# Experts take 96 rows as three 32-column strips of plain float32 weights on TensorE's four column tiles, with no split of expert slabs and a 14-slab ring

## The reference, cut to what matters

```
logits = (h @ w_router) + b_router
top_v, top_i = lax.top_k(logits, 2)
gates = softmax(top_v)
for e in range(8):
    y = (silu(h @ w1[e]) * (h @ w3[e])) @ w2[e]     # w1, w3: 1024 x 3584, w2: 3584 x 1024
    out = out + dense_gate[..., e:e+1] * y
```

## Time and profile before

| | us |
|---|---|
| median of three runs | 1696.49 |
| profiled execution, first to last instruction (span) | 1693.5 |
| time of that execution, as far as it is known: median less span | 3.0 around the span |
| ahead of the experts | 713.1 |
| eight experts | 713.1 to 1672.0 |
| behind the experts | 21.5 |

### The profile page before, as it was taken

How to read it: one execution, slowest core, us unless ns; L and a number is a source line. 1 busy time by engine, 2 the same in 40 slices (tenths; PEclk the granted TensorE clock), 3 DMA queues, 4 the chain that set the end, 5 groups by cost and what they waited for, 6 DMA issues and landing times.

```text
span 1693.5 us, 22933 instructions
## 1 busy us (share of the span) xinstructions
PE 1587.1 (94%) x8697; PEld 1295.9 (77%) x8697; DVE 1255.3 (74%) x1097; ACT 982.6 (58%) x885; POOL 153.9 (9%) x135
## 2 busy tenths in 40 slices
PE   6889999799899887899999999999999999999996
PEld 3579999498785574488888888888888888888874
DVE  4355543578782834488898888988888888889996
ACT  2244432433322633277777877877877877777774
POOL 0000000025541511200000000000000000000210
PEclk9789999899999988599999999999999999999998
DMA  9895555855458428689999999999999999999991
GB/s 345 295 346 177 180 160 183 299 174 194 155 212 305 141 75 333 214 320 382 359 389 384 355 395 364 380 387 379 370 391 367 378 386 364 382 386 363 394 386 49
DMA packets 248254, 512.28 MB, mean 302 GB/s; under 512 B 9046, under 2 KB 68614, under 8 KB 248176
## 3 DMA queue, kind: packets, MB, share of 16 engines
q1 hardware_dynamic: 241015, 490.27, 80.6%
q0 software_dynamic: 4768, 16.89, 2.5%
q10 hardware_dynamic: 2400, 4.17, 0.7%
HBM read 498.19 MB, written 13.82 MB: 302 GB/s over the span
## 4 chain that ended last, share of the span: by engine, by line
PE 76%; DVE 9%; DMA 5%; POOL 3%; ACT 3%; issue 3%; SPq 1%; DVEq 0%; ACTq 0%; POOLq 0%
PE wide L474 22%; PE wide L475 22%; PE wide L476 22%; DVE w_lo L1729 2%; POOL phase L1907 2%; DMA ring<-in_ada_mix_w 2%; DVE phase L1570 2%; DMA ring<-in_ada_ffn_w 1%; PE wide L930 1%; POOL phase L1913 1%; ACT w_hi L1262 1%; PE wide L525 1%; PE wide L536 1%; SPq L437 1%; DMA ring<-in_cache_v 1%
## 5 line engine op out<-in xcount | busy, mean ns | idle before, releaser
L1729 DVE TENSOR_TENSOR w_lo<-ring,w_hi 128x2048 fp32r<-128x2048 f32 x336 | 767.6, 2290 | 114.0 <-ACT w_hi L1262 112.5
L1262 ACT ACTIVATE w_hi<-ring 128x2048 fp32r<-128x2048 f32 x336 | 643.6, 1919 | 216.5 <-PE wide L476 214.3
L474 PE MATMUL wide<-w_hi,xe_hi 128*128 128x512 f32 x896 | 355.7, 397 | 5.6 <-DVE w_lo L1729 2.9
L475 PE MATMUL wide<-w_lo,xe_hi 128*128 128x512 f32 x896 | 350.2, 391 | 0.0
L476 PE MATMUL wide<-w_hi,xe_lo 128*128 128x512 f32 x896 | 350.2, 391 | 0.0
L474 PE MATMUL wide<-tHi,w_hi 128*128 128x264 f32 x672 | 198.3, 295 | 20.4 <-DVE mLo L1488 20.4
L404 DVE TENSOR_TENSOR w_lo<-ring,w_hi 128x2048 fp32r<-128x2048 f32 (+1 forms) x58 | 139.0, 2399 | 101.2 <-ACT w_hi L1002 100.9
L475 PE MATMUL wide<-mLo,w_hi 128*128 128x264 f32 x736 | 212.3, 288 | 0.0
L474 PEld LDWEIGHTS wide<-w_hi,xe_hi 128*128 128x128 f32 x896 | 169.0, 189 | 45.1 <-DVE w_lo L1729 8.6
L476 PEld LDWEIGHTS wide<-w_hi,xe_lo 128*128 128x128 f32 x896 | 168.8, 188 | 35.8
L475 PEld LDWEIGHTS wide<-w_lo,xe_hi 128*128 128x128 f32 x896 | 169.0, 189 | 33.4
(11 more groups left out here) (313 smaller groups left out, 1709.8 us busy)
## 6 DMA issues: line engine op xcount, KB each, us to landing
ring<-in_moe_w SPq DMA_DIRECT2D x336, 1024.0 KB, 7.4
ring<-in_ffn_w SPq DMA_DIRECT2D x30, 1024.0 KB, 5.4
ring<-in_ada_mix_w SPq DMA_DIRECT2D x24, 1024.0 KB, 8.8
ring<-in_ada_ffn_w SPq DMA_DIRECT2D x24, 1024.0 KB, 12.0
ring<-in_w_q SPq DMA_DIRECT2D x12, 1024.0 KB, 9.1
ring<-in_cache_k SPq DMA_DIRECT2D x24, 512.0 KB, 4.9
ring<-in_cache_v SPq DMA_DIRECT2D x24, 512.0 KB, 6.3
ring<-in_w_kv SPq DMA_DIRECT2D x8, 1024.0 KB, 6.5
```

Source lines behind the costliest of these rows:

```text
L474: pe.matmul(out, a[0], b[0], start=start, stop=False, skip_group_check=True)
L475: pe.matmul(out, a[0], b[1], start=False, stop=False, skip_group_check=True)
L1262: act.activation(w_hi[:, (NSPLIT + k) % PAIRS, :], ring[:, slot, :], ACT.Copy).then_inc(hi_done, 1)
L1729: dve.tensor_tensor(w_lo[:, i, :], ring[:, slot, :], w_hi[:, i, :].bitcast(F32), ALU.subtract).then_inc(lo_done, 1)
```

## The change

SLOTS goes from 128 to 96, and the 96 rows of an expert are three strips of 32. PASSES stays 3, as 264/96 rounds up to 3, and the flag's bound becomes 96.5. Experts' weights are no longer split: TensorE reads the plain float32 slabs. A group is four matmuls with the same 128x32 stationary strip; each takes a quarter of the slab's columns and writes one of four 32-partition tiles of a bank.

w1 and w3 are taken in two parts, columns 0-2047 (four times 512) and 2048-3583 (four times 384); w2 in slabs of 256 rows by 1024 columns (four times 256). An expert has 38 slabs: 16 of 1 MB, 8 of 1.5 MB, 14 of 1 MB; a row of a slab is 8, 6 or 4 KB long in DRAM, where it was 2 KB (w1, w3) or 4 KB (w2). The ring for them is 14 MB: the room of w_hi, w_lo, the old ring and xT, in one piece.

```
-SLOTS = 128
+SLOTS = 96
+STRIPS = SLOTS // 32
+PARTS = ((0, 512), (2048, 384))
+UNITS = 56
...
+    eslabs = [(m, 0, k) for m in (1, 3) for k in range(KC)] + [(m, 1, k) for m in (1, 3) for k in range(KC // 2)]
+    eslabs += [(2, 0, k) for k in range(FE // (2 * P))]
...
+                def product(m, part):
+                    first, n = 0 if m == 1 else STRIPS, PARTS[part][1]
+                    for k in range(KC):
+                        i, kk = eslabs.index((m, part, k // (part + 1))), k % (part + 1)
+                        if kk == 0:
+                            landed(i)
+                        for s in range(STRIPS):
+                            for j in range(4):
+                                mm = pe.matmul(bank[first + s][32 * j:32 * (j + 1), 0:n], xe[:, k, 32 * s:32 * (s + 1)], expert_slab(i)[:, kk, n * j:n * (j + 1)],
+                                               start=(k == 0), stop=(k == KC - 1))
+                        if kk == part:
+                            mm.then_inc(expert_used, 1)
+                        if (m, part, k) == (1, 1, 1):
...
+                            turn(0, 0, 6)
+                            turn(0, 1, 7)
...
+                def down():
+                    pe.wait_ge(upT_ready, count(2 * STRIPS, STRIPS))
+                    for i in range(FE // (2 * P)):
...
+                        for half in range(2):
...
+                            for s in range(STRIPS):
+                                for j in range(4):
+                                    mm = pe.matmul(bank[6 + s // 2][32 * j:32 * (j + 1), 256 * (s % 2):256 * (s % 2 + 1)], block[:, 32 * s:32 * (s + 1)],
+                                                   expert_slab(k)[:, half, 256 * j:256 * (j + 1)], start=(f == 0 and s % 2 == 0), stop=(f == FE // P - 1),
+                                                   skip_group_check=True)
...
+                pe.wait_ge(xe_ready, count(1, 1))
+                product(1, 0)
+                product(3, 0)
+                pe.wait_ge(silu_done, count(2 * STRIPS, STRIPS))
+                product(1, 1)
+                pe.wait_ge(up_ready, count(2 * STRIPS, STRIPS))
+                product(3, 1)
+                down()
...
+                def silu(part):
+                    act.wait_ge(expert_used, used(e, c, eslabs.index((1, part, KC // (part + 1) - 1))))
+                    for s in range(STRIPS):
+                        act.activation(gated_up[part][:, s, :], bank[s][:, 0:PARTS[part][1]], ACT.Silu).then_inc(silu_done, 1)
...
-                dve.tensor_tensor(w_lo[:, i, :], ring[:, slot, :], w_hi[:, i, :].bitcast(F32), ALU.subtract).then_inc(lo_done, 1)
...
-                act.activation(w_hi[:, (NSPLIT + k) % PAIRS, :], ring[:, slot, :], ACT.Copy).then_inc(hi_done, 1)
...
-                    pool.dma_start(slab_rows(y_rows, e, c), ye[:, :]).then_inc(y_stored, 16)
-                    pool.wait_ge(y_stored, 16 * (done + 1 - min(c, 1)))
+                    for j in range(4):
+                        pool.dma_start(slab_rows(y_rows, e, c)[:, 256 * j:256 * (j + 1)].rearrange("(s t) n -> t s n", t=32),
+                                       ye[32 * j:32 * (j + 1), :].rearrange("p (s n) -> p s n", s=STRIPS)).then_inc(y_stored, 16)
+                    pool.wait_ge(y_stored, 64 * (done + 1 - min(c, 1)))
```

More of the change, by code:

```diff
@@ L29 @@
 FE = 3584
-FCH = FE // 512
 EPS = 1e-6
@@ L114, in yoco_step, with occupant, slot @@
     ada_order = {n: i for i, n in enumerate(ada_slabs)}
[L116 to L119, removed]
-    PER_E = len(eslabs)
-    assert PER_E % RING == 0 and PER_E % PAIRS == 0
-    assert all(plan[n][0] not in ("ck", "cv") for n in range(NPRE - RING, NPRE))
+    eslabs = [(m, 0, k) for m in (1, 3) for k in range(KC)] + [(m, 1, k) for m in (1, 3) for k in range(KC // 2)]
+    eslabs += [(2, 0, k) for k in range(FE // (2 * P))]
+    units = [6 if part else 4 for m, part, k in eslabs]
+    begins = [sum(units[:k]) for k in range(len(eslabs))]
+    def occupant(k):
+        last = (begins[k] + units[k] - 1 - UNITS) % (3 * UNITS)
+        found = [i for i in range(len(eslabs)) if begins[i] <= last < begins[i] + units[i]][0]
+        return found if found < k else found - len(eslabs)
+    PER_E = len(eslabs)
+    begin_slots = [b % UNITS // 4 for b in begins]
+    assert sum(units) == 3 * UNITS
+    assert all(plan[n][0] == "ada" for n in range(NPRE - RING, NPRE))
+    def slot(n):
+        return (n - NPRE) % RING
     with ExitStack() as ctx:
@@ L272, in yoco_step @@
[L272 to L295, removed]
+        gated_up = [at(8192, STRIPS, 512), at(8192, STRIPS, 384)]
@@ L882, in _ @@
             pe.wait_ge(ht_taken, KC)
-            pe.matmul(bank[2][:, 0:P], ones, before, start=True, stop=True).then_inc(count_row, 1)
+            pe.matmul(bank[2][:, 0:P], ones, before, start=True, stop=True).then_inc(counts_summed, 1)
             pe.wait_ge(gate_rows, 1)
@@ L926, in turn @@
[L926 to L930, removed]
-                    mm.then_inc(up_turned, 1)
[L933 to L942, removed]
-                                mm = three(bank[6 + q][0:SLOTS, :], (upT_hi[j % 2][:, 2 * half + i, :], upT_lo[j % 2][:, 2 * half + i, :]),
-                                           (hi[:, i, cols], lo[:, i, cols]), j == 0 and half == 0 and i == 0, j == FCH - 1 and half == 1 and i == 1)
-                        mm.then_inc(pair_used, 1)
-                        if half == 0 and between is not None:
-                            turn(between)
@@ L949, in expert @@
-                pe.wait_ge(xe_ready, count(1, 1))
-                for j in range(FCH):
-                    pe.wait_ge(silu_done, count(FCH, j + 1))
-                    product(1, j, 3)
-                    if j >= 1:
-                        turn(j - 1)
-                    pe.wait_ge(up_ready, count(FCH, j + 1))
-                    product(3, j, 4)
-                    if j >= 1:
-                        down(j - 1, between=(j if j == FCH - 1 else None))
-                if not last:
-                    turn_rows(e, c, 1)
@@ L1855, in expert @@
+                if last and c == 0:
+                    for q in range(3):
+                        early_sum(q)
+                gate_up(0)
+                gate_up(1)
+                if not last:
+                    rows_taken(e, c, 1)
+                dve.wait_ge(expert_used, used(e, c, PER_E - 1))
                 dve.wait_ge(y_free, count(1, 1))
-                dve.tensor_copy(ye[0:SLOTS, 512:1024], bank[7][0:SLOTS, :]).then_inc(y1_copied, 1)
+                dve.tensor_copy(ye[:, 512:768], bank[7][:, 0:256]).then_inc(y1_copied, 1)
```

318 lines of the change are left out of this document (165 added, 153 removed).

## The result

The changed kernel takes 3663.43 us (median, 3660.81 to 3668.41), 2.160 times the time before (95% interval 2.157 to 2.163); forecast were 3580, 3450 to 3800. Its profiled execution has a span of 3660.8 us. From the changed kernel's page: the busy line, the DMA of the 40 slices, the weight queue (q1) and instruction queue (q8) with packets and MB, and the chain.

A forecast was written before the change was run, and what follows sets the result against it. TensorE was taken to bound the experts. Terms: 713.1 + 3 x 909.6 + 3 x 2.5 + 52.5 + 16.5 + 58 = 3576.4 us of span, plus 3.0, so 3580 us, 2.11 times the time before; range 3450 to 3800.

The forecast's parts named there:

- Three passes: Whole kernel: expert 2's 113 rows exceed 96.5, so passes 1 and 2 run too; at TensorE's pace, chance 0.80.
- one pass: Rival at the flag: fullest expert has 96 rows or fewer, flag not set, 1650 us, 2.7% faster; chance 0.05.
- strips that drain: Rival in the experts: groups cost an isolated one's 1.06 us, 149.9 us an expert, 4450 us; chance 0.05.
- loads that bind: Rival in the experts: weight queues give no more than 366 GB/s, 120.3 us an expert, 3738 us; chance 0.09.
- drain rival: Non-streaming groups, chance 0.05; cited the skill's 79% of ideal for three column tiles beside 0.86 of 1.06, 81%.
- start of the experts: Ahead of the experts: 713.1 us stays, near 2 us won on VectorE's chain and a hop, 1 to 2 lost.
- 24 experts without waits: Three passes of eight experts: 113.7 us each on TensorE, from 108.4 to 119.5.
- gap pass 0 to 1: TensorE idle for copies, merge, flag, memset, clears, scatter and rows in: 52.5 us, from 30 to 80.
- gap pass 1 to 2: Between the passes, copies, store, three more issues, rows in and turned: 16.5 us, from 10 to 25.
- behind pass 2: Tail of copies, store, memset, six gathers, six additions, norm and output: 58 us, from 45 to 75.
- rest of the passes: Start of each pass: a cool clock adds 2.5 us, three times.
- No wait is put on top: In each expert: SiLU, gated product and copies lie beside 15 to 20 us of another product, adding nothing.

The follow-up runs named there:

- e1: Changed kernel with the flag's bound at 128.5, so one pass runs and 17 pairs of expert 2 are left out; 1687.35 us.
- e2: Kernel before with only the flag's bound moved from 128.5 to 96.5, so three passes run; 3689.16 us in one execution.
- e3: Changed kernel with PASSES = 2, all 528 pairs computed; 2696.26 us, 1.589 times the time before.
- e4: Changed kernel with one pass (17 pairs left out), seven experts written out on TensorE in place of the loop; 1646.2 us.
- e5: Changed kernel with one pass (17 pairs left out), TensorE's loop body rotated so the jump stands behind product(1, 0); 1685.42 us.
- e11: Kernel before with three experts in the body of TensorE's loop, two turns, one jump back; 1698.34 us, ratio 1.0017.
- e13: Kernel before with two experts in the body of TensorE's loop, three turns, two jumps back; 1695.65 us in a single execution.

## Why the prediction was right, and where its terms were off

**Three passes: right.** Expert 2's 113 rows set the flag, and e1, e2 and e3 show that the passes make the time. All three rivals fell: one pass (three stages), strips that drain (0.65 and 0.44 us a group in a stretch of 100 us), loads that bind (401 GB/s in e4 with TensorE never idle). The 81% in the drain rival is another ratio than the 79% beside it: it sets a streamed group against an isolated one, and no run here shows tiles one after another.

The sum was 84.4 us of span too low, 3576.4 for 3660.8. That the time still lies in the range is in part luck: the room above the sum was left for dear transposes and for slow loads, and was filled by waits that the sum put at nothing. By its terms (one expert is e4's, the 1.7 is read at one jump):

| term | forecast | measured | difference |
|---|---|---|---|
| start of the experts | 713.1 | 708.3 | -4.8 |
| 24 experts without waits | 24 x 113.7 | 24 x 112.53 | -28 |
| jumps back, idle | 0 | 90.2 | +90 |
| lower clock behind them | 0 | 18 x 1.7 | +31 |
| early sums in pass 0, lower clock behind | 0 | 12.2 + 2.9 | +15 |
| gap pass 0 to 1 | 52.5 | 49.4 | -3 |
| gap pass 1 to 2 | 16.5 | 15.5 | -1 |
| behind pass 2 | 58 | 40.8 | -17 |
| rest of the passes, their starts at a lower clock in it | 3 x 2.5 | 10.2 | +2.7 |

**The failed sentence is "No wait is put on top".** I took the gap-free stream of the old expert for a property of the loop; it was one of the loop's length. The diff shows what counts: from 540 matmuls of one record to 720 of two for an expert, with a weight load for each record: some 1080 records a turn became 2938. The second miss stands in the same sentence: I looked at what ScalarE and VectorE do for this product, not at what VectorE has queued ahead of it in the last expert.

**One expert: right to 1%.** 112.53 against 113.7, inside the bounds of 108.4 to 119.5.

**The start: a net gain was there.** The scatter began 6.7 us earlier (681.86 against 688.59) but took longer, so the first rows were asked for only 2.3 us earlier (702.41 against 704.66); from there to the first product it took 5.9 us, not 8.5. VectorE's two split jobs left the chain; that these 5 us are theirs is argued, not tested. And the nine transposes of the gate matrix (2.53 us) lie ahead of the wait for the rows, beside GpSimd's scatter.

**Gap of pass 0 to 1: right in sum, by misses that cancel.** GpSimd's timeline of the changed kernel:

```profile
1672.86 0.95 POOL L2031 MEMSET mT<- 128x1024 f32 x1 [83.64 <-issue]
1674.10 8.04 POOL L1961 DMA_DIRECT2D x_rows<-mT  x16 [0.29 <-POOL mT L2031]
1701.12 1.08 POOL L1966 DMA_INDIRECT x_rows<-phase,row  x1 [18.98 <-DMA x_rows<-mT]
...
1709.88 0.57 POOL L2002 DMA_DIRECT2D hT<-x_rows  x1 [1.43 <-DMA x_rows<-phase,row]
```

The clears took 27.0 us from first issue to the scatter, not 18; the scatter 8.8, not 16, with only 17 pairs that have a row in the second table; reading the flag 1.1 (merge ended at 1671.77), not 3.7.

**Behind pass 2: mis-sized by 17 us.** The rows of the changed kernel's GpSimd that answer to the earlier trace rows, VectorE's first addition, and for comparison a gather of the same kernel's first pass:

```profile
3621.11 2.15 POOL L2023 DMA_DIRECT2D y_rows<-mT  x4 [109.32 <-ACT mT L1351]
3625.25 5.22 POOL L1984 MEMSET ring<- 128x6144 f32 x1 [1.99 <-DMA y_rows<-mT]
3631.29 1.09 POOL L1988 DMA_INDIRECT ring<-y_rows,row  x1 [0.83 <-POOL ring L1984]
...
3637.86 0.91 POOL L1988 DMA_INDIRECT ring<-y_rows,row  x1 [0.30 <-issue]
```

```profile
3640.15 1.29 DVE L1897 SCALAR_TENSOR_TENSOR mT<-ring,phase,mT 128x1024 f32<-128x1024 f32 x1 [19.61 <-DMA ring<-y_rows,row]
```

```profile
1552.39 1.10 POOL L1977 DMA_INDIRECT hT<-y_rows,row  x1 [0.83 <-POOL hT L1974]
```

The store landed 4.1 us after its first issue, not 8.1; a gather is issued every 1.3 us, not 2.2; the last landed 2.3 us after its issue began, not 6.5. For the store the rows point at traffic: the same four issues, beside weights at the end of expert 6, were waited for 6.74 us behind the last one, here 1.99. For the gathers' issue it is not traffic: in the first pass's last expert a gather takes 0.9 to 1.1 us to issue as well, at 378 to 417 GB/s. There VectorE and ScalarE are idle; beside the 1.9 to 2.6 us of the kernel before they were busy 83 to 87% and 68 to 83%, with the split. No run changes their load alone, so that cause stays open. And the last gathers move 17 rows (0.07 MB) over queues without weights, those of the earlier trace rows 1.91 MB beside them; which of the two makes the landing short isn't separated. Memset, additions and norm came within 1.3 us of their prices.

## What to carry to other kernels

Before a tile is made smaller, find the fullest load that it must hold and the price of overflow: 17 rows too many cost two passes here. When a change multiplies the instructions in a hardware loop, count them, and look in the instruction queue for a body that is fetched anew on each turn: here each jump back of such a loop cost 1 to 6 us of idle TensorE, and behind the longer gaps a lower clock. Written out, the loop cost neither. A price holds for the load beside which it was read: ask which engines and queues were busy there, and whether they still are.

## What the hardware showed

- A jump back of TensorE's loop shows no idle time at some 1080 records in the body, 1.0 us at 2160, 2.4 at 3240 (full-width float32r) and 5.0 at 2938 (strips). Each time the work resumes 2.6 to 2.9 us after the start of a 16 KB packet in the instruction queue.
- Behind a gap of 5.00 us (e1) TensorE lost 1.7 us to the clock, with 0.50 (1.2 GHz) granted from 829 to 832; behind one of 3.84 us (e5) 2.9 us, with 0.50 from 849 to 854. Behind 2.41 us (e11) the clock was 0.57 in 1073 to 1077; behind 0.94 and 1.07 us (e13) it stayed at 1.00. A shorter gap did not always mean a smaller loss.
- One core's queues carried 401 GB/s over a whole expert of e4.
- A gather of GpSimd took 0.9 to 1.1 us to issue with 378 to 417 GB/s in the queues and VectorE and ScalarE idle (changed kernel, first pass), and 1.9 to 2.6 us at 385 to 388 GB/s with VectorE busy 83 to 87% (kernel before).
